# Branch c's attention scores for four steps at once, and two transposed buffers exchanged

## The reference, cut to what matters

```python
h = rms_norm_2(x, g_mix[l])
proj = h @ w_in[l]
c_q, c_kv, k_r, qkv_b, qkv_c, gate_logits = split(proj)
y_a = mla_mixer(...)              # 8 heads
y_b = dilated_mixer(...)          # 12 heads, masks
y_c = neighbourhood_mixer(...)    # 8 heads, 64 wide, with a bias: softmax(q k * scale + bias) v
gates = sigmoid(gate_logits)      # 3 x 1024
merged = gates_a * (y_a @ w_pa) + gates_b * (y_b @ w_pb) + gates_c * (y_c @ w_pc)
x = x + merged @ w_o[l]
x = x + (silu(h @ w1) * (h @ w3)) @ w2
```

## Time and profile before

| | |
|---|---|
| median of 3 runs | 1535.86 us (1535.68 to 1536.5) |
| the profiled execution's own time | 1535.41 us |
| its span, first to last instruction | 1533.7 us |
| TensorE, matmuls | 1522.7 us busy, 99% |
| vector engine | 1096.0 us busy, 71% |
| scalar engine | 802.2 us busy, 52% |
| TensorE's mean granted clock | 0.998 |

### The profile page before, as it was taken

The page is one execution under the profiler, slowest core; times in us unless marked ns, Lnnn a source line. Parts: engine busy times, 40 slices in busy tenths (PEclk is TensorE's granted clock), DMA queues, the critical chain, the costliest instruction groups (busy, mean ns, idle before and its releaser), DMA issues.

```text
span 1533.7 us, 19837 instructions
## 1 busy us (share of the span) xinstructions
PE 1522.7 (99%) x8182; PEld 1293.3 (84%) x8182; DVE 1096.0 (71%) x1374; ACT 802.2 (52%) x948; POOL 40.1 (3%) x36
## 2 busy tenths in 40 slices
PE   9999999999999999999999999999999999999997
PEld 7888888888888888888887888888888887888886
DVE  5778666676786666977757886667877758876666
ACT  6646444456564454765445364544665445464444
POOL 0100000001000000002000100000002000100000
PEclk9999999999999999999999999999999999999999
DMA  9525555554255554445343455554444433555551
GB/s 314 196 106 197 187 197 190 190 193 165 104 199 190 195 192 160 160 147 185 138 151 124 184 196 197 193 178 168 172 156 163 146 123 138 206 206 192 178 203 59
DMA packets 44281, 265.95 MB, mean 173 GB/s; under 512 B 6048, under 2 KB 9248, under 8 KB 14368
## 3 DMA queue, kind: packets, MB, share of 16 engines
q1 hardware_dynamic: 41504, 262.02, 47.7%
q10 hardware_dynamic: 2688, 2.67, 0.7%
HBM read 263.63 MB, written 1.05 MB: 173 GB/s over the span
## 4 chain that ended last, share of the span: by engine, by line
PE 97%; DVE 1%; DMA 0%; SPq 0%; issue 0%; ACT 0%; DVEq 0%
PE psum L578 21%; PE psum L482 18%; PE psum L484 18%; PE psum L483 18%; PE psum L587 11%; PE psum L520 5%; PE psum L959 1%; PE psum L890 1%; PE psum L912 1%; PE psum L950 1%; PE psum L897 1%; DVE wl L1476 1%; DMA raw<-in_weights 0%; PE psum L748 0%; PE psum L732 0%; DVE work L2016 0%
## 5 line engine op out<-in xcount | busy, mean ns | idle before, releaser
L1476 DVE TENSOR_TENSOR wl<-raw,wh 128x2048 fp32r<-128x2048 f32 (+1 forms) x245 | 550.8, 2251 | 220.2 <-ACT wh L1061 220.1
L1061 ACT ACTIVATE wh<-raw 128x2048 fp32r<-128x2048 f32 (+2 forms) x249 | 465.8, 1874 | 320.8 <-PE psum L484 196.2
L482 PE MATMUL psum<-wh,xhl 128*128 128x512 f32 (+2 forms) x928 | 365.6, 394 | 0.5 <-DVE xhl L1704 0.4
L484 PE MATMUL psum<-wh,xhl 128*128 128x512 f32 (+2 forms) x928 | 357.6, 385 | 0.0
L483 PE MATMUL psum<-wl,xhl 128*128 128x512 f32 (+2 forms) x928 | 356.8, 385 | 0.0
L578 PE MATMUL psum<-xhl,wh 128*128 128x512 f32 x1408 | 336.6, 391 | 0.0
L578 PEld LDWEIGHTS psum<-xhl,wh 128*128 128x128 f32 x1408 | 261.2, 188 | 52.3
L482 PEld LDWEIGHTS psum<-wh,xhl 128*128 128x128 f32 x928 | 174.4, 188 | 36.9 <-issue 3.8
L484 PEld LDWEIGHTS psum<-wh,xhl 128*128 128x128 f32 x928 | 174.3, 188 | 34.8
L483 PEld LDWEIGHTS psum<-wl,xhl 128*128 128x128 f32 x928 | 174.6, 188 | 31.6
L587 PEld LDWEIGHTS psum<-xhl,wl 128*128 128x128 f32 x1408 | 175.3, 192 | 3.7
(11 more groups left out here) (196 smaller groups left out, 1236.0 us busy)
## 6 DMA issues: line engine op xcount, KB each, us to landing
raw<-in_weights SPq DMA_DIRECT2D x233, 1024.0 KB, 4.8
raw<-in_weights SPq DMA_DIRECT2D x10, 512.0 KB, 3.8
raw<-in_weights SPq DMA_DIRECT2D x4, 832.0 KB, 4.3
raw<-in_weights SPq DMA_DIRECT2D x12, 256.0 KB, 7.2
work<-in_rpb ACTq DMA_DIRECT2D x4, 438.0 KB, 8.0
raw<-in_weights SPq DMA_DIRECT2D x2, 768.0 KB, 4.2
out<-arena SPq DMA_DIRECT2D x3, 256.0 KB, 3.0
x<-in_x SPq DMA_DIRECT2D x4, 128.0 KB, 3.6
```

Of the source, the lines that this page charges most:

```text
L482: nc.tensor.matmul(dst, lh, right(wh, slot), start=start, stop=False)
L484: return nc.tensor.matmul(dst, ll, right(wh, slot), start=False, stop=stop)
L1061: nc.scalar.activation(wh[:, slot, 0:n], raw[:, slot, 0:n], ACT.Copy).then_inc(high_ready.sem, 1)
L1476: nc.vector.tensor_tensor(wl[:, slot, 0:n], raw[:, slot, 0:n], wh[:, slot, 0:n].bitcast(F32), ALU.subtract).then_inc(split_ready.sem, 1)
```

## The change

Turns 12 and 13 become one turn (steps 22 and 23), and branch c scores two turns at a time: step 15 scores turns 9 and 10, step 19 scores turns 11 and 12, and steps 17, 21 and 22 score nothing. For this the second pair of a row tile gets two banks of its own (ACC + 2 and ACC + 3) and buffers of its own for the biased scores, the probabilities and the transposed probabilities.

TensorE: the weighted sums of branch c's first row tile are not made at step 21 any more but together with the second's at step 22, right behind the transposes of steps 22 and 23; those of the last two steps wait for the copies of these transposes one by one. Piece 34's projection is no longer interrupted. New waits: `o_free` 3 at step 15, `o_free` 4 at step 19, and the maximum of turn 10 ahead of branch b's last weighted sums at step 17.

Scalar engine: the exponentials of turn 10 move to step 16, behind `split_high(30)`; those of turns 11 and 12 both stand at step 19, ahead of branch a's high parts and of step 20's tanh. The copy of branch c's first output moves from step 21 to step 23.

Vector engine: `row_max` 10 and `unit_sums` 10 at step 16; at step 19 the copies, `row_max` 11, `split_low(32)`, `unit_sums` 11, `row_max` 12, branch a's low parts, `split_low(33)`; `unit_sums` 12 at step 20; `split_low(35)` at step 21, ahead of the merge of piece 33, and `split_low(36)` at step 22.

Branch b: steps 8, 9, 14 and 15 use the buffer in `work` and steps 10 to 13 the one in `arena`, so that step 9 copies its transposes before it copies the output of branch a's second row tile.

The core of the diff:

```diff
 TURNS = [(0,), (1,), (2, 3), (4, 5), (6, 7), (8, 9), (10, 11), (12, 13), (14, 15)] + \
-    [(16, 17), (18, 19), (20, 21), (22,), (23,)]
+    [(16, 17), (18, 19), (20, 21), (22, 23)]
-TRANSPOSES_FIRST = range(8, 22)
-MAXIMUM_FIRST = range(17, 23)
+TRANSPOSES_FIRST = range(8, 24)
+SCORES_AT = {15: (TURN_ENDING[17], TURN_ENDING[19]), 17: (), 19: (TURN_ENDING[21], TURN_ENDING[23]), 21: (), 22: ()}
+SOFTMAX_AT = {15: (TURN_ENDING[17],), 16: (TURN_ENDING[19],), 17: (), 19: (TURN_ENDING[21], TURN_ENDING[23]),
+              21: (), 22: ()}
...
-        biased_c = part(arena, 3072, 1024)
+        biased_c = [part(arena, 3072, 1024), part(arena, 4096, 1024)]
+        prob_c = [part(arena, 5120, 1024), part(arena, 6144, 1024)]
...
+        def transposed_b(m):
+
+            return prob_t_b[1 if m in (8, 9, 14, 15) else 0]
...
# TensorE, weighted(u)
-                    if j < 3:
+                    if j < 3 or last == 19:
                         return
-                    pe.wait_ge(*tr_free.by(L, TR2["pt", u] + (3 if kind == "b" else len(TURNS[u]))))
+                    copied = TR2["pt", u] + (3 if kind == "b" else 0 if kind == "c" else len(TURNS[u]))
+                    pe.wait_ge(*tr_free.by(L, copied))
+                    if last == 15:
+                        pe.wait_ge(*max_ready.by(L, TURN_ENDING[19] + 1))
...
+                        if m in (22, 23):
+                            pe.wait_ge(*tr_free.by(L, copied + m - 21))
...
# TensorE, turn(m)
-                    if m == 21:
-                        probs_t(u)
-                        scores(u + 1)
-                        weighted(u - 1)
-                        return
                     attend(u)
+                    if m == 22:
+                        weighted(u)
...
-                    scores(u + 1)
+                    for scored in SCORES_AT.get(m, (u + 1,)):
+                        scores(scored)
...
# scalar engine
-                    if m + 1 < STEPS and m in TURN_AT and m not in (2, 22):
-                        softmax_exp(TURN_AT[m] + 1)
...
+                    for u in SOFTMAX_AT.get(m, (TURN_AT[m] + 1,) if m in TURN_AT and m != 2 else ()):
+                        softmax_exp(u)
...
# vector engine
+                    if m == 16:
+                        row_max(TURN_ENDING[19])
                     if u is not None:
...
-                        if m not in MAXIMUM_FIRST:
+                        if m < 16 or m == 19:
                             row_max(u + 1)
...
-                    if u is not None:
-                        unit_sums(u + 1)
+                    for softmax in SOFTMAX_AT.get(m, (u + 1,) if u is not None else ())[0:1]:
+                        unit_sums(softmax)
+                    if m == 19:
+                        row_max(TURN_ENDING[23])
+                    if m == 20:
+                        unit_sums(TURN_ENDING[23])
                     if m == 21:
                         split_low_half(L, 34, 1)
+                        split_low(L, 35)
                     if m == 22:
-                        branch_c_low(0)
+                        split_low(L, 36)
```

More of the change, by code:

```diff
@@ L60 @@
 TURNS = [(0,), (1,), (2, 3), (4, 5), (6, 7), (8, 9), (10, 11), (12, 13), (14, 15)] + \
[L61 removed]
+    [(16, 17), (18, 19), (20, 21), (22, 23)]
 TURN_ENDING = {steps[-1]: u for u, steps in enumerate(TURNS)}
[L63 to L65 removed]
+TURN_AT = {m + (m == 1) - (m == 23): u for m, u in TURN_ENDING.items()}
+TRANSPOSES_FIRST = range(8, 24)
+SCORES_AT = {15: (TURN_ENDING[17], TURN_ENDING[19]), 17: (), 19: (TURN_ENDING[21], TURN_ENDING[23]), 21: (), 22: ()}
+SOFTMAX_AT = {15: (TURN_ENDING[17],), 16: (TURN_ENDING[19],), 17: (), 19: (TURN_ENDING[21], TURN_ENDING[23]),
+              21: (), 22: ()}
 N1, FFN1 = 51, 18
@@ L403, in transposed, with pair_in_c, prob_of @@
             if kind == "b":
-                return prob_t_b[j // 2][:, (j % 2) * 768:(j % 2 + 1) * 768]
-            return part(arena, 5120 + 512 * j, 512) if m >= 20 else prob_t4[j]
+                return transposed_b(m)[:, (j % 2) * 768:(j % 2 + 1) * 768]
+            return part(arena, 7168 + 512 * j, 512) if m >= 20 else prob_t4[j]
         def o_bank(kind, t):
             return bank(ACC + 3 if kind == "b" else ACC + 2 + t)
+        def pair_in_c(u):
+            return step_kind(TURNS[u][0])[2] // 2
+        def prob_of(u):
+            return prob_c[pair_in_c(u)] if step_kind(TURNS[u][0])[0] == "c" else prob
         def heads_of_turn(u):
@@ L896, in scores @@
                             rows = slice(64 * hh, 64 * hh + 64)
-                            mm = nc.tensor.matmul(bank(ACC + hh)[:, (i // 2) * SEQ:(i // 2 + 1) * SEQ],
+                            mm = nc.tensor.matmul(bank(ACC + 2 * pair_in_c(u) + hh)[:, (i // 2) * SEQ:(i // 2 + 1) * SEQ],
                                                   c_t[rows, j, t * P:(t + 1) * P], c_t[rows, 4 + j, :],
@@ L924, in probs_t @@
                     else:
-                        blocks = [prob[:, b * P:(b + 1) * P] for b in range(4 * len(TURNS[u]))]
+                        blocks = [prob_of(u)[:, b * P:(b + 1) * P] for b in range(4 * len(TURNS[u]))]
                     for i in tiles or range(len(blocks) // 4):
@@ L938, in weighted @@
                             pe.wait_ge(*free.by(L, 9))
-                    for m in (last - 2, last) if kind == "b" else range(last - 3, last + 1):
+                    for m in {"a": range(last - 3, last + 1), "b": (last - 2, last), "c": range(16, STEPS)}[kind]:
                         kind, t, j = step_kind(m)
+                        if m in (22, 23):
+                            pe.wait_ge(*tr_free.by(L, copied + m - 21))
                         if j == (1 if kind == "b" else 0):
@@ L1016, in _ @@
                         pe.wait_ge(*xl_ready.by(L, 9))
-                        project(L, q, 19 + q - 32, 0, between=between, at=(1, 1))
+                        project(L, q, 19 + q - 32, 0)
                     if m == 0:
                         latent_t(TR2["ak_rest"] + 2, ak_tok, (3,))
-                    if m < STEPS - 1 and m in TURN_AT and m != 2:
+                    if m in TURN_AT and m != 2:
                         turn(m)
@@ L1352, in softmax_exp @@
                             src = bank(ACC + i // 2)[:, (i % 2) * SEQ:(i % 2 + 1) * SEQ] if kind == "a" else \
-                                biased_c[:, i * SEQ:(i + 1) * SEQ]
+                                biased_c[pair_in_c(u)][:, i * SEQ:(i + 1) * SEQ]
                             ins = nc.scalar.activation(
-                                prob[:, i * SEQ:(i + 1) * SEQ], src, ACT.Exp, bias=smax[:, i:i + 1],
+                                prob_of(u)[:, i * SEQ:(i + 1) * SEQ], src, ACT.Exp, bias=smax[:, i:i + 1],
                                 scale=A_SCALE if kind == "a" else 1.0, accum_out=den[:, at + i:at + i + 1])
@@ L1397, in _ @@
                             act.dma_start(bias_runs[r * 64:(r + 1) * 64, :, :], src).then_inc(bias_in.sem, 16)
-                    if m in (2, 22):
+                    if m == 2:
                         softmax_exp(TURN_AT[m] + 1)
-                    if m == 22:
+                    if m == STEPS - 1:
+                        act.wait_ge(*o_full.by(L, 5))
+                        nc.scalar.activation(y_t["c"][:, :, 0:P], part(bank(ACC + 2), 0, 4, P), ACT.Copy, scale=0.5)\
+                            .then_inc(o_free.sem, 1)
                         branch_c_high(0)
@@ L1971, in row_max @@
                             rev = part(bias[:, 2 * j + hh, :], at, 4, GRID_W)[:, :, ::-1]
-                            two = part(psum[:, ACC + hh, :], (i // 2) * SEQ, 4, GRID_W)
+                            two = part(psum[:, ACC + 2 * pair_in_c(u) + hh, :], (i // 2) * SEQ, 4, GRID_W)
                             ins = nc.vector.tensor_tensor_reduce(
-                                part(biased_c, i * SEQ, 4, GRID_W), two, rev, 1.0, LOWEST, ALU.add, ALU.max,
+                                part(biased_c[pair_in_c(u)], i * SEQ, 4, GRID_W), two, rev, 1.0, LOWEST, ALU.add, ALU.max,
                                 smax[:, 4 + i:5 + i])
@@ L1987, in unit_sums @@
                     heads = prob_b if kind == "b" else \
-                        [prob[:, i * SEQ:(i + 1) * SEQ] for i in range(2 * len(TURNS[u]))]
+                        [prob_of(u)[:, i * SEQ:(i + 1) * SEQ] for i in range(2 * len(TURNS[u]))]
                     at = 32 + 4 * t + j if kind == "b" else (0 if kind == "a" else 16) + 8 * t + 2 * j
@@ L2043, in _ @@
                     if q >= 32:
[L2045 to L2048, removed]
+                        if m == STEPS - 1:
+                            v.wait_ge(*o_free.by(L, 5))
+                            output(5)
                         merge(q, (35 - q) // 2, (q - 32) % 2, 20 + q - 32,
-                              between={22: lambda: row_max(u + 1), 23: last_lows}.get(m))
+                              between=(lambda: branch_c_low(0)) if m == STEPS - 1 else None)
```

(18 more changed lines are left out.)

10 lines of the change are left out of this document (5 added, 5 removed).

## The result

The changed kernel takes 1545.69 us (median, 1545.42 to 1545.99), the kernel before 1535.88: ratio 1.0063, 95% interval [1.0046, 1.0081]. It is slower by 9.8 us; the forecast was 11.4 more, 1547.3. The profiled execution has a span of 1544.1 us, 10.4 more than before.

The account below looks back on a forecast made before the run. TensorE, busy for 99% of the span, was taken as the bound; stalls of 4.4, 1.9 and 0.5 us less 1.0 gained and 0.1 already waited make +5.7 us a layer, +11.5 for two: 1547.3 us (range 1543.0 to 1551.5).

Parts of the forecast that it names:

- Step 19's chain: From step 19's burst through maxima, sums and exponentials to step 20's tanh: TensorE waits 4.4 us a layer before project 32.
- B: Start of step 19's burst on TensorE, the zero from which the prediction counts its times.
- Step 21: Before project 33: TensorE waits 1.9 us a layer for merge 32, which stands behind split 34's first half and unit sums 12.
- the hole of 1.9 us: Expected sign in the changed profile: TensorE idle about 1.9 us before project 33, ended by the vector engine's merge.
- Step 22: In step 22's burst: last weighted sums wait 0.5 us a layer for copies, with split 35 ahead of merge 33.
- The gains: TensorE's attention bursts at steps 15 to 23 and project 34 left uncut: about 1.0 us a layer saved.
- My sum of +5.7: Whole stage, per layer: stalls 4.4, 1.9 and 0.5 us, less 1.0 gained and 0.1 already waited at project 32.
- Rival (1): Clock falls in the hole before project 32, slowing matmuls 0 to some 4 us a layer: 1547.5 to 1555 us; chance 0.18.
- Rival (2): No stall before project 32, only fewer bursts: 1.0 us a layer saved, 1533.9 us; chance 0.05.
- Rival (3): Only the stall before project 32 shows, the later waits are covered: +3.4 us a layer, 1542.7 us; chance 0.12.
- The edits costed at nothing: Turn 10's softmax work at step 16, step 15's output wait and branch b's buffer exchange at step 9: 0 us.
- The chain behind project 34: From project 35 on, branch c's lows, merge 35 and split 37 keep their offsets: no added cost.

Follow-up runs that it names:

- e3: Changed kernel with separate columns for maxima and reciprocals of steps 22 and 23, so both row maxima adjoin: 1539.67 us.
- e5: Changed kernel with 18 extra matmuls, results unused, in the hole ahead of project 32: 1545.98 us.
- e8: e4 with the second half of split 34 moved behind step 22's copies: 1532.87 us.
- e6: Changed kernel with only e4's vector-engine edit (merge 32 and step 21's copies ahead of unit sums 12 and split 34, split 35 later): 1545.99 us.
- e7: e6 with e5's 18 extra matmuls in the hole ahead of project 32: 1541.91 us.
- e4: Changed kernel with e2's edit plus vector order: merge 32 and copies ahead of unit sums 12 and split 34, split 35 behind step 22's copies: 1533.77 us.
- e1: Kernel before with only the exchange of branch b's two transposed buffers: 1536.0 us.
- e2: Changed kernel with the exponentials of steps 22 and 23 behind step 20's tanh on the scalar engine: 1545.13 us.

## Why the prediction was right, and where its sizes were off

**Step 19's chain.** Right in every link, to 0.1 us. Exponentials 11 at B + 3.85 (forecast 3.85), unit sums 11 at 5.97 (6.05), row maximum 12 at 7.24 (7.32), exponentials 12 at 8.93 (9.02), tanh at 11.95 (12.05), project 32 at 12.76 (12.86). The wait is 4.15 us in the view, forecast 4.4; counted by starts, as the forecast was, it is 4.31, for the view counts the end of the last matmul as busy. e3 shows that the second maximum's place decides most of it.

**Step 21.** Project 33 at B + 18.3, forecast 18.4. Merge 32 frees the bank when it was told to, but the hole of 1.9 us that was named as a sign does not show in the changed kernel: project 32 at the low clock made TensorE just as late. Only e3 and e5, at full clock, show the wait, 1.6 us in the view and 1.86 by starts in e5 (forecast 1.9).

**Step 22.** 0.2 us for a copy, forecast 0.5, and in layer 0 alone; project 34 at B + 26.3 and, in layer 1, 26.5, forecast 26.5.

**The gains** are the term that was too small. I counted 1.0 us a layer; e8 shows 1.4. From step 15's burst to step 19's the changed kernel is 0.34 us shorter in layer 0 (790.70 to 819.75 against 790.48 to 819.87 before) and 0.32 in layer 1, where I had 0.2: the two bursts changed by +0.87 and -1.07 as counted, and the four projects between them are quicker by 0.14 and 0.11 us together, which I had not counted and for which no run shows a cause. The 64 weighted records take 3.68 us in e8 (835.66 to 839.34) where I had 3.80. From project 34 on, 84 matmuls take 19.2 us in the changed kernel (846.02 to 865.22). My sum of +5.7 had 5.58 and the 13.96 of before (845.99 to 859.95) for them, 19.5, and left out the 0.1 that I had listed among the gains; in e8 they take 19.4.

From step 13's burst to the transposes behind project 37's first half, the trace is 5.05 us longer than before in layer 0 and 5.33 in layer 1; the forecast, not rounded, was 5.76. In layer 0 the difference is 0.14 at steps 15 to 18, 0.23 in project 34's start and 0.34 behind it; in layer 1 it is 0.12, nothing and 0.32.

**Rival (1), the clock,** came about in both layers, which I had given 0.18, but not its price. I had set it at 1547.5 to 1555, about 1550; it cost 0 in layer 0 and some 0.3 us in layer 1. I had seen that the wait for the merge would hide a part, and should have kept to it: the merge makes TensorE wait for 1.86 us by starts (e5), and project 32 and its transposes are slower by 1.87 us in layer 0. That the two are so nearly equal is luck: in layer 1 the slow clock reaches 0.6 us beyond the cover. So the waits were foreseen; that the clock, which the forecast had at full, would fall and cost so little was not. e6 and e7 show what it costs without cover. My 2.83 us for twelve matmuls at 1.2 GHz were too many: e6 has 2.4. The Trainium skill, "TensorE: Matmul & The Clock Gate", Part 1, says that an idle stretch throttles the array; the traces agree for holes of 4.15 us (clock 0.62 in the window behind it) and show no fall for those of 1.1 and 1.6 us in e3 and 1.6 in e5 (1.00 in the windows of the stage).

**Rival (2), no stall,** did not happen, but e4 and e8 are the kernel in which it does: 1533.9 forecast for it, 1533.77 and 1532.87 measured. **Rival (3)**, the first stall only, did not happen: the second wait does not show, but the low clock stood in its place and the time was not 1542.7.

**The edits costed at nothing.** The exchange of the buffers: e1, nothing. Steps 15 to 17: no hole. The chain behind project 34: none either.

## What to carry to other kernels

Where one engine is full and others have idle time, count the start of its next job, not the average: a chain over two engines (maximum, exponential, sums, maximum, exponential) must fit between two bursts, and what stands behind it in the same engine's order, here a tanh that frees a bank, is late by all of it. When work is joined for TensorE's sake, the other engines' orders have to be written anew with it: mending the scalar engine's alone moved the hole (e2), mending the vector engine's alone laid the low clock bare (e6), and only both together won (e4). A buffer can stretch such a chain too: columns of their own for the second maxima were worth 6 us (e3). A hole can be hidden in another wait, and so can a low clock, so an experiment that takes away one of them can show nothing though the cost is real.

## What the runs showed of the hardware that was not expected

In both layers, and in e2 and e6 as well, the granted clock fell at a hole of 4.15 us, to 1.2 GHz (0.50). The moment differs between layers of one kernel. In layer 1 of the changed kernel the clock is low before project 32 starts, as a window and the start show:

```profile
1291.00:1293.00 2.00, 0.59 (x2) 0.52 (x3) 1.79 (x3) 2.00 (x5) 0.00 (x0) 0.50 0.00 0
```

```profile
1292.41 0.77 PE L499 MATMUL psum<-wh,ah 128*128 128x512 f32 x1 [4.15 <-ACT work L1410]
```

In layer 0 it falls about 1 us behind the hole's end, with TensorE already at work again: project 32's first four matmuls are followed by the next after 0.23 to 0.31 us and only the later ones after 0.40 to 0.43. What decides the moment is not shown. Eighteen matmuls in the hole, whose results nobody used, kept the clock at 2.4 GHz (1.00 in e7's windows). That was worth 4.1 us in e7 and nothing that can be measured in e5.
